# Loads ahead of the activation store in the feed-forward of a hybrid decoder step

## The reference

```python
  h = RMSNorm(x); z = h @ w_in            # then windowed attention and mLSTM heads
  x = x + concat(A, B) @ w_out
  x = x + W_down( silu(causal_dwconv3(h2 W_gate)) * (h2 W_up) ),  h2 = RMSNorm(x)
```

## Time and profile before

| | us |
|---|---|
| median of three runs | 2363.3 |
| the profiled execution | 2364.5 |
| its span | 2362.7 |
| TensorE busy | 2253.2 |
| VectorE busy | 1620.8 |
| ScalarE busy | 899.3 |
| GpSimd busy | 1034.6 |

### The profile page before, as it was taken

How to read it: one execution, slowest core, us unless ns; L and a number is a source line. 1 busy time by engine, 2 the same in 40 slices (tenths; PEclk the granted TensorE clock), 3 DMA queues, 4 the chain that set the end, 5 groups by cost and what they waited for, 6 DMA issues and landing times.

```text
span 2362.7 us, 34413 instructions
## 1 busy us (share of the span) xinstructions
PE 2253.2 (95%) x13423; PEld 1984.9 (84%) x13423; DVE 1620.8 (69%) x2271; ACT 899.3 (38%) x1524; POOL 1034.6 (44%) x811
## 2 busy tenths in 40 slices
PE   7999999999999998888879999989999999999999
PEld 6899878887777888777768999988999998888887
DVE  5666655556573457888878899888998974445653
ACT  4555622222232324444444444444444433233331
POOL 4333312222121346655554666655666630245730
PEclk9999999999999998999998999999999999999999
DMA  8433222222154553444344333353333345686454
GB/s 283 151 126 121 79 86 81 81 81 67 45 183 142 192 184 122 156 139 138 132 161 140 117 118 116 118 181 100 119 118 119 119 158 190 219 289 202 139 177 165
DMA packets 208076, 333.95 MB, mean 141 GB/s; under 512 B 23083, under 2 KB 148679, under 8 KB 205847
## 3 DMA queue, kind: packets, MB, share of 16 engines
q1 hardware_dynamic: 207883, 331.69, 41.5%
q0 software_dynamic: 32, 0.07, 0.0%
HBM read 235.42 MB, written 97.24 MB: 141 GB/s over the span
## 4 chain that ended last, share of the span: by engine, by line
PE 65%; DVE 7%; DMA 5%; issue 4%; POOL 3%; ACT 3%; SPq 0%; DVEq 0%; POOLq 0%; ACTq 0%
PE bank L114 12%; PE bank L115 12%; PE bank L116 12%; PE bank L2803 9%; PE bank L2804 8%; PE bank L2805 8%; DMA late_c_raw<-in_w_ffn_in_dram 3%; DVE late_t L3184 1%; DVE late_s_act L3154 1%; DVE late_t_lo L3129 1%; POOL late_c_raw L3381 1%; POOL late_t_raw L3385 1%; DVE late_t L3187 1%; DMA late_a_raw<-h_parts 1%; ACT late_t_hi L2930 1%
## 5 line engine op out<-in xcount | busy, mean ns | idle before, releaser
L2803 PE MATMUL bank<-late_a_hi,late_b_hi 128*128 128x384 f32 (+1 forms) x1056 | 350.0, 331 | 56.3 <-issue 18.6
L2804 PE MATMUL bank<-late_a_lo,late_b_hi 128*128 128x384 f32 (+1 forms) x1056 | 344.7, 326 | 0.0
L2805 PE MATMUL bank<-late_a_hi,late_b_lo 128*128 128x384 f32 (+1 forms) x1056 | 343.2, 325 | 0.0
L2803 PE MATMUL bank<-late_a_hi,late_t_hi 128*128 128x384 f32 (+1 forms) x792 | 262.9, 332 | 19.6 <-DVE late_gp L3172 8.5
L2803 PEld LDWEIGHTS bank<-late_a_hi,late_b_hi 128*128 128x128 f32 x1056 | 201.7, 191 | 69.1 <-issue 36.3
L2804 PE MATMUL bank<-late_a_lo,late_t_hi 128*128 128x384 f32 (+1 forms) x792 | 258.3, 326 | 0.0
L2805 PE MATMUL bank<-late_a_hi,late_t_lo 128*128 128x384 f32 (+1 forms) x792 | 257.6, 325 | 0.0
L114 PE MATMUL bank<-late_e_hi,late_y_a_hi 128*128 128x512 f32 x616 | 242.1, 393 | 2.1 <-DVE late_e_lo L3202 2.1
L116 PE MATMUL bank<-late_e_hi,late_y_a_lo 128*128 128x512 f32 x616 | 242.6, 394 | 0.0
L115 PE MATMUL bank<-late_e_lo,late_y_a_hi 128*128 128x512 f32 x616 | 241.7, 392 | 0.0
L3379 POOL TENSOR_TENSOR late_t_raw<-late_c_raw 128x512 f32<-128x512 f32 x64 | 84.2, 1315 | 327.9 <-DMA late_c_raw<-in_w_ffn_in_dram 300.4
(11 more groups left out here) (380 smaller groups left out, 5187.1 us busy)
## 6 DMA issues: line engine op xcount, KB each, us to landing
late_c_raw<-in_w_ffn_in_dram SPq DMA_DIRECT2D x64, 1024.0 KB, 5.1
late_y_a_raw<-act_parts SPq DMA_DIRECT2D x77, 512.0 KB, 3.6
late_e_raw<-in_w_down_dram SPq DMA_DIRECT2D x77, 256.0 KB, 4.1
act_parts<-late_s_act SPq DMA_DIRECT2D x22, 768.0 KB, 4.4
att_next_hh<-h_parts SPq DMA_DIRECT2D x16, 1024.0 KB, 4.8
late_d_raw<-in_w_down_dram SPq DMA_DIRECT2D x11, 1024.0 KB, 7.6
late_a_raw<-h_parts SPq DMA_DIRECT2D x14, 768.0 KB, 12.7
act_parts<-late_t SPq DMA_DIRECT2D x22, 384.0 KB, 2.5
```

The lines of the kernel that those rows point to most:

```text
L2803: nc.tensor.matmul(out, w_h, hi[:, c, :], start=first, stop=False, skip_group_check=True)
L2804: nc.tensor.matmul(out, w_h, lo[:, c, :], start=False, stop=False, skip_group_check=True)
L2805: ins_ = nc.tensor.matmul(out, w_l, hi[:, c, :], start=False, stop=last, skip_group_check=True)
```

## The change

- SyncE: `load_b(1, after(r))` is issued ahead of `store_act(before(r))`. In the last round of a group the first two loads of `load_next_a` stand before it and the other five behind it, all ahead of the store.
- `load_next_a` for group 1: the first slot waits for the earlier stores of the tokens instead of a product, the others for the product that last used the bytes that they overwrite; ScalarE's `round_a` waits for the products that last used its own destination.
- First round: VectorE makes `combine(r, 0, 2)` before the splits of unit 1, and the first split of the next round before two taps. `pair_s(final)` and `store_s(final)` come a round later.
- Last round: ScalarE rounds the first operand of the down projection before the last `silu`, VectorE splits it before `combine(r, 1, 3)`.

```diff
--- before.py
+++ after.py
@@ -2569,12 +2569,18 @@
             sp.dma_start(a_dram[3:7, i, :, cols].rearrange("m p n -> p m n"),
                          s_act[:, 0:4 * G.PH].rearrange("p (m n) -> p m n", m=4)).then_inc(landed, 16)
 
-        def load_next_a(G):
+        def load_next_a(G, slots):
 
             last = (groups[G.index - 1], NP - 1)
-            free = (6, 9, 10, 12, 13, 13, 13) if G.index == 1 else range(7, 14)
-            for slot in A_ORDER:
-                w_prod(sp, last, free[slot])
+            free = (None, 7, 8, 9, 11, 12, 13) if G.index == 1 else range(7, 14)
+            for slot in slots:
+                if free[slot] is None:
+                    w_h_out(sp, final)
+                    w_s_out(sp, final.pair)
+                    x1_out.wait(sp, final)
+                    x1_out.wait(sp, final - 1)
+                else:
+                    w_prod(sp, last, free[slot])
                 if slot in (A11, A12, A22):
                     part, col = slot != A11, G.base + G.H * (slot == A22)
                     src = h2_dram[:, 0, part * KH:(part + 1) * KH, col:col + G.H]
@@ -2690,25 +2696,22 @@
                     load_b(0, after(r))
                     if before(r) != FIRST and before(r)[0].sample:
                         load_d(before(r))
+                    turning = i == NP - 1 and r != LAST
+                    if turning:
+                        load_next_a(groups[G.index + 1], A_ORDER[:2])
+                    load_b(1, after(r))
+                    if turning:
+                        load_next_a(groups[G.index + 1], A_ORDER[2:])
                     if r == LAST:
                         load_turn(0)
                     store_act(before(r))
-                    load_b(1, after(r))
-                if G.index == 0 and i == 1:
+                if G.index == 0 and i == 2:
                     store_s(final)
                 if G.index == 1 and i == 0:
                     store_conv_s()
                     load_acc_s()
                 if G.index == 1 and i == 2:
                     store_y_s()
-                if i == NP - 1 and r != LAST:
-                    H = groups[G.index + 1]
-                    if G.index == 0:
-                        w_h_out(sp, final)
-                        w_s_out(sp, final.pair)
-                        x1_out.wait(sp, final)
-                        x1_out.wait(sp, final - 1)
-                    load_next_a(H)
         for n in range(1, RINGS):
             load_turn(n)
         store_act(LAST)
@@ -2916,6 +2919,8 @@
                 act.wait_ge(a_summed, 4)
             else:
                 act.wait_ge(a_in[slot], 16 * G.index)
+                if G.index == 1 and slot != S4:
+                    w_prod(act, (groups[0], NP - 1), (8, 9, 10, 12, 13, 13)[slot])
             nc.scalar.activation(A_hi(slot, G), A_raw(slot, G), ACT.Copy).then_inc(a_rounded, 1)
 
         def round_b(r, u, q):
@@ -3041,9 +3046,11 @@
             keep_first(r, 1, 1)
             if late_a:
                 round_a(nxt[0], 0)
+            if nxt is None:
+                round_turn(0)
             silu_of(r, 1)
             if nxt is None:
-                for n in range(RINGS):
+                for n in range(1, RINGS):
                     round_turn(n)
             round_b(nxt, 0, 1)
             round_b(nxt, 0, 2)
@@ -3230,11 +3237,13 @@
             combine(r, 0, 1)
             if turned:
                 split_a(G, 6)
+            if p is not None:
+                split_b(r, 1, 2)
+            combine(r, 0, 2)
             if p is None:
                 split_b(r, 1, 0)
                 split_b(r, 1, 1)
-            split_b(r, 1, 2)
-            combine(r, 0, 2)
+                split_b(r, 1, 2)
             split_b(r, 1, 3)
             combine(r, 0, 3)
             if p is not None and p[0].sample:
@@ -3249,7 +3258,9 @@
                 combine(r, 1, 1)
                 tap(r, 0, 2)
                 combine(r, 1, 2)
-                if p is not None:
+                if p is None:
+                    split_b(nxt, 0, 0)
+                else:
                     split_d(p, 1)
                 sum_act(p, 2)
                 sum_act(p, 3)
@@ -3267,12 +3278,13 @@
                 tap(r, 1, 1)
                 combine(r, 1, 2)
                 tap(r, 1, 2)
-            split_b(nxt, 0, 0)
+            if p is not None:
+                split_b(nxt, 0, 0)
             if late_a:
                 split_a(nxt[0], 0)
-            combine(r, 1, 3)
             if nxt is None:
                 split_turn(0)
+            combine(r, 1, 3)
             split_b(nxt, 0, 1)
             split_b(nxt, 0, 2)
             if late_a:
@@ -3428,7 +3440,7 @@
                 heads(r)
             tails(r)
             sums_b(after(r), 0)
-            if p is None:
+            if p == FIRST:
                 pair_s(final)
 
         def sum_e(n):
```

## The result

The changed kernel takes 2387.7 us, the median of four runs (2384.3 to 2391.6), against 2363.8 us (2362.5 to 2365.5) for the kernel before in the same comparison: a ratio of 1.010 (95% interval 1.008 to 1.012). The forecast of 2353 us and its range are missed, on the side of the rival "Slower". The profiled execution took 2384.3 us, its span is 2382.6 us.

What follows compares the result with a forecast made beforehand. Group 0 rounds (30.9 us) were bound by a ring with `load_b(1)` late behind `store_act`; TensorE was full in groups 1 and 2. -5.7 + 12.2 - 8 - 5 - 3.7 = -10.2 from 2364.5: 2354.3, median 2353; range 2318 to 2371.

Steps and rivals of the forecast that it cites:

- Slower: Rival, chance 0.15: collision at the end of unit 1 outweighs everything; group 0 rounds of 34 us, 2371 us in all.
- The order of events: Group 0: `load_b(1)` issued right after `split_b(r,1,3)`, GpSimd's `sums_b(r,1)` at the end of unit 1; right in any case.
- the size of a meeting: Group 0, end of unit 1: VectorE loses 1.03 and 0.91 us per GpSimd instruction met, 3.9 us for four.
- the first rounds: Group 0's start: `combine(r,0,2)` and a split moved earlier, `pair_s` a round later; 5.7 us gained, bounds 2 and 8.
- the turns: Changes of group, loads issued earlier: group 0 to 1 gains 8 us (2 to 15), 1 to 2 gains 5 (2 to 11).
- the end: First turn of the down projection: `round_turn(0)` and `split_turn(0)` moved earlier; gain 3.7 us, bounds 2 and 4.
- -3.6 of idle time, +3.9 of collision: Group 0 round: VectorE's idle time goes, GpSimd's sums collide; with TensorE's 0.8, +1.1 us, 32.0 instead of 30.9.
- 0.8 for TensorE: Group 0 round: clock TensorE may lose by waiting longer between units; bounded by 0 and 3 us, taken as 0.8.
- Groups 1 and 2: 0, TensorE is full there, and GpSimd's sums already start as unit 1 ends: Feed-forward rounds of groups 1 and 2: the early load changes nothing, 0 us; TensorE busy 148.6 of 149.0 us.
- 2 us a round before it would show: Groups 1 and 2: reserve if the cover went, as VectorE has 27.6 us of work in 29.8 us rounds.
- The ring was all: Rival, chance 0.20: collision falls into gaps, group 0 rounds go to 28.5 us; 2322 us in all.
- The clock: TensorE at its lower clock after longer idle in group 0 rounds, as at 920.40; cost counted in the 0.8 us.

Runs made afterwards that it cites:

- the first experiment: Changed kernel with only the early load undone: `store_act` again ahead of `load_b(1)` in every round but a group's last; 2347.9 us, ratio 0.994.
- the fills: Changed kernel with GpSimd's four sums of unit 1 replaced by zero fills of the same buffers, so less work than the reference; 2318.0 us, ratio 0.982.

## Why the prediction was wrong

**What held.** The order of events (early load, sums at the end of unit 1), the size of a meeting (3.9 us forecast for four sums, 4.1 measured on the four tap instructions: 1.04, 1.02, 1.02 and 1.00), and the first rounds, the turns and the end: -22.4 us forecast, -18.6 read from the traces (4.0, 7.1, 3.5 for the second turn's window, 4.0), -15 by the first experiment.

**The step that failed: a round of group 0.** It was "-3.6 of idle time, +3.9 of collision" and 0.8 for TensorE, "since VectorE and not TensorE sets the pace": +1.1 us. Measured: +2.25 in the ordinary rounds, and 10 us more in four long ones. The sum took idle time anywhere in the round against work in one part of it. A round is a ring: end of unit 1, VectorE's taps and splits, the combine that TensorE waits for last, then 17.6 us of TensorE to the next end. All of the taps' collision lies in the first part of it. Of the idle time only 1.8 us was won, not 3.6: VectorE now waits 0.87 and 0.53 us for banks that TensorE fills late and 0.40 us for the down weights. Its idle time in one round went from 5.2 us before (30.85 less 25.6) to 3.4 (33.1 less 29.7), while its busy time rose by 4.1. 4.1 less 1.8 is the 2.3 us.

Two meetings were missing from my list. The gates follow the sums, so they too start earlier in the round, by 6.4 and 4.2 us, and they lengthen two splits inside the ring by 2.5 us, where they used to meet two later ones of unit 1 (the 1.91 us of the earlier trace rows is one). The experiment that moved them shows their share at the end: 0.5 us a round, because TensorE is the next limit at once. And `load_d`, which I had not costed, is late now in some rounds; putting it first gives 6 us back, 8 of the 29.6 in its stretch.

**The other step that failed: "Groups 1 and 2: 0, TensorE is full there, and GpSimd's sums already start as unit 1 ends".** They didn't: GpSimd stood 9.28 us for the load before its sum at 1374.31, by which time VectorE had finished the split at 1373.42. The late load kept GpSimd off VectorE. Without it one split takes 1.79 instead of 0.69 us, TensorE waits 0.51 us a round, and the two groups lose 5.8 and some 7.2 us (+3.7 from D to E, with the 3.5 that the turn's window gave). The row of one round would have shown it; I read only the busy share, and a share of 99.7% says nothing of what a wait there would cost. My reserve of "2 us a round before it would show" failed too: it was VectorE's idle time over the whole round, and 0.76 us on the way to one `combine` was enough. The run with the wait in group 0 only shows the loss in group 1 again (307.5 us against 299.6).

**The rivals.** "Slower" named the right mechanism and the right point to decide it, 33.2 us a round, and had 34 us for its rounds: +24 us by its terms up to T10, +25.6 measured. It missed groups 1 and 2, and they are 13 of the 17 us by which the time lies above 2371, the upper end of my range. (The lower end, 2318, doesn't come out of my own bounds: the ring at 2322 with turns of 15 and 11 is 2309.) I gave it 0.15 for the reason that TensorE "has slack before VectorE": it had 3.66 us of waits in a round (0.65, 0.54, 0.81, 1.25, 0.41). The first grew to 4.56, and the other four shrank to 0.40 and 0.34: 3.9 us more against 2.3 given back. "The ring was all" wasn't wrong in what a round can do: with the wait for the third split and the rounding moved up, rounds go to 29.0, where it had 28.5.

**The clock** was not it in the ordinary rounds. Two ordinary rounds of the kernel after, one with a granted clock of 0.90 and one with 0.95, took the same 33.1 us (the windows; TensorE's busy time is 27.8 and 27.0):

```profile
1079.20:1112.30 33.10, 27.81 (x183) 25.79 (x181) 29.72 (x35) 13.35 (x19) 18.13 (x16) 0.90 0.37 124
1046.10:1079.20 33.10, 27.00 (x183) 24.98 (x181) 29.71 (x34) 13.35 (x19) 18.17 (x16) 0.95 0.37 124
```

In the second TensorE started at its full level and waited longer at the next splits, 0.66 us at 1057.25 and 0.88 at 1061.59, where the first has 0.40 and 0.34. In these rounds the lower level costs nothing, since VectorE's chain is later anyway; from 1079.2 to the `combine` at 1094.06 it waits for nothing of TensorE's.

**What collides.** The Trainium skill ("SBUF — State Buffer", section "SBUF: two separate sides") says that a VectorE instruction with two SBUF inputs contends only with a GpSimd instruction that reads SBUF. The taps at 0.74 us beside the fills, against 1.79 beside the sums, agree. Its exclusive lock for the whole instruction fits in kind again, and not in size: 1.0 us on each tap beside sums of 1.26 to 1.62 us.

## What to carry to other kernels

A late transfer can be what keeps two engines from meeting. Before one moves it up, one should list what its consumer will now run beside, instruction by instruction, in every stage that shares the code, and everything queued behind that consumer. And a collision is priced by whether it lies between the event that starts it and the one that this ring waits for next: the same four sums, held back by one wait on the third split, turn a loss of 1.0% into a gain of 1.1%.

## What the runs showed of the hardware

- Where VectorE's instruction finds one of GpSimd's running, what it costs depends little on how long VectorE's own is: a tap of 64 columns goes from 0.28 to 1.30 us, one of 512 from 0.75 to 1.79, a split of 1024 from 1.22 to 2.17 or 2.30. It is about 1.0 us for a GpSimd sum that has just begun and 1.25 beside a gate.
- The engine that comes second pays. In the feed-forward of the kernel after, 31 splits of 1024 columns were already running when GpSimd's next `TENSOR_TENSOR` started, and all took 1.21 to 1.23 us, as alone; 102 started while one of GpSimd's was running and took 1.63 to 2.84. The kernel before has both sides of it: the split at 1017.85 finds only the end of a sum (1016.81 to 1018.10) and takes 1.33 us, and the sum that starts at 1018.18, with the split running, takes 2.15 us; the same sum of unit 0, at 1031.57, takes 1.35.
- GpSimd pays too: the second and fourth sum take 1.6 us beside the taps and 2.15 beside the 1024-column splits, where the taps leave the first and third at 1.3.
- GpSimd's zero fill of 128x512 takes 0.53 us, and the taps beside it stay at 0.74 us.
